# Routing start of a hybrid attention/mLSTM/MoE layer: out-projection tail in column quarters, split top-k, single bias products

## The chip, the cores and the metric

The kernel runs on one core of a Trainium2 chip, in float32. The metric is the device time of one execution in microseconds (us). The kernel before took 1073.36 us, the median of 3 runs (1073.18 to 1074.63).

## The reference, cut to what matters

One layer over 256 tokens (two tiles of 128, t = 0 and 1) of width 1024. Attention and mLSTM give `mixed`; then:

```python
x = x + jnp.einsum('bse,ed->bsd', mixed, w_out[l])               # the out-projection
h = rmsnorm(x, norm2_g[l])
logits = jnp.dot(h, w_router) + b_router                         # 32 experts
top_v, top_e = lax.top_k(logits, 4)
gates = jax.nn.softmax(top_v, axis=-1)
# each expert e, on the tokens that chose it:
gu = jnp.dot(xb, w_gate_up[e]) + b_gate_up[e]                    # 1024 -> 2048
act = min(gu[:, :1024], 7) * sigmoid(1.702 * gate) * (clip(up) + 1)
y = jnp.dot(act, w_down[e]) + b_down[e]                          # 1024 -> 1024
x = x + sum of gate * y
```

The weights of the 32 experts are 32 times (8.39 + 4.19) MB = 402.7 MB, each read once.

## The kernel before, in words

Weights pass through `ring`, 12 pieces of 2 MB in SBUF. An expert takes four gate/up pieces (`load_gu`, L398) and two down pieces (`load_d`, L410). All are issued by SyncE in one fixed order; from expert 2 on each issue waits until TensorE has used the piece that held the slot (`gu_used`, `d_used`). Experts 0 and 1 are loaded while the mixer still runs. The last two pieces of expert 1 go to slots 10 and 11, which hold the second half of `w_out` and the turned activations `ht`: slot 10 waits for `mixed` 4 (all of the out-projection done), slot 11 for `logit_parts` 2 (`ht` read). Then comes the bias row of expert 2 (`load_brow`, L402, behind `brow_used`), and then the first gate/up piece of expert 2, behind `gu_used` 1. That semaphore rises when TensorE has done the first two k blocks of expert 0's gate/up products (L1493).

The stretch that the change touches lies between the mixer and that product. Order on TensorE (PE), written out by hand: `out_half(t, c, ks)` (L1311) multiplies tile t by column half c of `w_out`, 512 columns a product; the first four k blocks of all four halves are done earlier, k 4 to 7 from 141 us. Between them `turn_x(t, i)` (L1333) transposes four 128-column blocks of the new x. Then `logit_part` (L1344) forms the router logits: eight k blocks go to four 32-row strips of one bank as 32-wide products, the strips are copied out (`part_copy`, ScalarE L713), and `fold_parts` (L1354) adds them by one product with a folding matrix. `tint_first(h)` (L1362) starts bank h with expert 0's gate/up bias, two one-row products each. Then the ranks (L1387, L1388, L1391), one product whose result nobody reads (L1389), `gather_first` (L1412: the picked tokens, eight products of 256 columns), `turn_rows` (L1433) and `gate_up` (L1493).

VectorE (DVE) adds the out-projection to x (`add_x`, L966), sums squares (L970), copies tile 1's transposed blocks (`turned_1`, L974), then runs for each tile the chain logits, MAX8, index, compare, reduce (L994 to L1004) that gives `mask`, and after both tiles `pos` (L1017) and `pick` (L1007) for each. ScalarE (ACT) squares (L693), takes Ln and Exp (L699, L701) for the norm factor `rs2`, copies tile 0's transposed blocks (L708) and the parts (L713), takes the softmax exponentials (L723), loads a table (L730) and copies the first half of the gathered rows (L732). Engines work in order, each instruction behind its waits.

Of the kernel before, what the change touches and what calls it, by code (L numbers as in the profile page):

```python
# [28 lines left out]
P = 128  # L29
# [81 lines left out]
def layer_kernel(nc, x, norm1_g, w_in, q_norm_g, k_norm_g, conv_w, conv_b, w_mq, w_mk, b_igate, b_fgate,  # L111
                 mh_norm_g, w_out, norm2_g, w_router, b_router, w_gate_up, b_gate_up, w_down, b_down,
                 attn_bias, out):
    with ExitStack() as ctx:
# [113 lines left out]
        ss2h = sb("ss2h", [P, T, 2])  # L228
        ss2 = sb("ss2", [P, T])
# [18 lines left out]
        ld_small = sem("ld_small")  # L248
# [10 lines left out]
        ld_g2 = sem("ld_g2")  # L259
# [14 lines left out]
        eps_ready = sem("eps_ready")  # L274
# [38 lines left out]
        m_arg1 = sem("m_arg1")  # L313
# [13 lines left out]
        mixed = sem("mixed")  # L327
        x1_ready = sem("x1_ready")
# [11 lines left out]
        top_found = sem("top_found")  # L340
        eq_ready = sem("eq_ready")
# [17 lines left out]
        fold_ready = sem("fold_ready")  # L359
# [36 lines left out]
        def _(sp):  # L396
# [24 lines left out]
            sp.dma_start(bif[:, 0:1], b_igate[0].rearrange("(h o) -> h o", o=1)).then_inc(ld_small, 16)  # L421
            sp.dma_start(bif[:, 1:2], b_fgate[0].rearrange("(h o) -> h o", o=1)).then_inc(ld_small, 16)
# [4 lines left out]
            for r, g in ((R_QG, q_norm_g), (R_KG, k_norm_g)):  # L427
                for i in range(2):
# [9 lines left out]
                         norm2_g[0].rearrange("(q p j) -> p q j", p=P, j=RUN)).then_inc(ld_g2, 16)  # L438
# [24 lines left out]
            sp.wait_ge(mixed, 4)  # L463
            load_d(1, 0, 10)
            sp.wait_ge(logit_parts, T)
# [97 lines left out]
        def _(act_e):  # L563
# [5 lines left out]
            for t in range(T):  # L569
                act.wait_ge(ld_x[t], 16)  # L570
                if t:
                    act.wait_ge(x_ms, t)
                act.activation(sq_x, xres[:, t, :], ACT.Square, accum_out=ss1[:, t:t + 1]).then_inc(x_ms, 1)
                act.wait_ge(x_ms, t + 1)
                act.wait_ge(eps_ready, 1)
# [120 lines left out]
            def rms_x(t):  # L696

                act.wait_ge(ss2_sum, t + 1)
                act.activation(rs2[:, t:t + 1], ss2[:, t:t + 1], ACT.Ln, scale=1.0 / D, bias=eps[:, 0:1]).then_inc(act_step, 1)  # L699
                act.wait_ge(act_step, 7 + t)  # L700
                act.activation(rs2[:, t:t + 1], rs2[:, t:t + 1], ACT.Exp, scale=-0.5).then_inc(x1_rs, 1)  # L701
# [3 lines left out]
            rms_x(0)  # L705
# [4 lines left out]
            def part_copy(t):  # L710

                act.wait_ge(logit_parts, t + 1)
                act.activation(part_t[:, t, :], bank[ACC[t]][:, 0:P], ACT.Copy).then_inc(part_read, 1)  # L713
# [79 lines left out]
        def _(dve):  # L793
# [10 lines left out]
            dve.memset(eps[:, :], EPS).then_inc(eps_ready, 1)  # L804
            dve.wait_ge(consts, 1)
            dve.tensor_reduce(fold[:, :], ident[:, :].rearrange("p (g e) -> p e g", e=NE), AX.X, ALU.add).then_inc(fold_ready, 1)
# [37 lines left out]
            dve.wait_ge(ld_small, 16 * 2)  # L844
# [57 lines left out]
            def decay(h):  # L902

                a_bc = bank[6 + h // 2][:, (h % 2) * SEQ:(h % 2 + 1) * SEQ]
                dve.tensor_scalar(e_m[:, h, 0:SEQ], a_bc, acol[:, 0, 0, h:h + 1], 0.0, ALU.subtract, ALU.max)\
                    .then_inc(m_arg1, 1)
                dve.wait_ge(m_arg1, h + 1)
# [60 lines left out]
            def sum_x(t):  # L968
                dve.wait_ge(x1_ss, 2 * t + 2)
                dve.tensor_tensor(ss2[:, t:t + 1], ss2h[:, t, 0:1], ss2h[:, t, 1:2], ALU.add).then_inc(ss2_sum, 1)  # L970

            def turned_1(i):
                dve.wait_ge(h2_turned, 3 + i)
                dve.tensor_copy(ht[:, 4 * i:4 * i + 4, P:SEQ], bank[6 + i][:, :].rearrange("p (k n) -> p k n", k=4))\  # L974
                    .then_inc(turned_x1, 1)


            dve.wait_ge(ld_wr, 32)
# [12 lines left out]
            for t in range(T):  # L991
# [7 lines left out]
                dve.max_index(top_i[:, t, :], top_v[:, t, :], lg[:, t, :]).then_inc(top_found, 1)  # L999
                dve.wait_ge(top_found, t + 1)  # L1000
                dve.tensor_tensor(eq[:, t], expert_no[:, :].unsqueeze(1).broadcast_to([P, TOPK, NE]),
                                  top_i[:, t, 0:TOPK].unsqueeze(2).broadcast_to([P, TOPK, NE]), ALU.is_equal).then_inc(eq_ready, 1)
                dve.wait_ge(eq_ready, t + 1)
                dve.tensor_reduce(mask[:, t, :], eq[:, t].rearrange("p j e -> p e j"), AX.X, ALU.add).then_inc(mask_ready, 1)  # L1004
            dve.tensor_scalar(nv0[:, :], top_v[:, :, 0], -1.0, None, ALU.mult).then_inc(top_ready, 1)
# [9 lines left out]
            for t in range(T):  # L1015
# [3 lines left out]
                take_half(0, t).then_inc((picked_t0, picked)[t], 1)  # L1019
            dve.wait_ge(top_exp, T)  # L1020
# [39 lines left out]
            def experts(base, flagged=None):  # L1060
                dve.wait_ge(xr_turned, base + 1)
                if flagged:
                    dve.wait_ge(ld_g2, 16)
# [37 lines left out]
        def _(pe):  # L1101
# [49 lines left out]
            pe.wait_ge(ld_vec, 16 * 8)  # L1151
# [157 lines left out]
            def out_half(t, c, ks):  # L1309
                for k in ks:  # L1310
                    mm = pe.matmul(bank[ACC[2 * t + c]][:, :], mix_t[:, k, t * P:(t + 1) * P], wout[k // 4][:, k % 4, c * BANK:(c + 1) * BANK],  # L1311
                                   start=(k == 0), stop=(k == KD - 1))
# [23 lines left out]
            def logit_part(t, half):  # L1336

                if t == 0 and half == 0:
                    pe.wait_ge(wr_ready, 1)
                    pe.wait_ge(x1_ready, 2)  # L1340
                pe.wait_ge((turned_x0, turned_x1)[t], half + 1)
                for g in range(4):
                    k = 4 * half + g
                    mm = pe.matmul(bank[ACC[t]][g * NE:(g + 1) * NE, 0:P], wr[:, k, :], ht[:, k, t * P:(t + 1) * P],  # L1344
                                   start=(half == 0), stop=(half == 1), skip_group_check=True)
                if half:
                    mm.then_inc(logit_parts, 1)

            def fold_parts(t):

                pe.wait_ge(part_read, t + 1)
                if t == 0:
                    pe.wait_ge(fold_ready, 1)
                pe.matmul(bank[ACC[t]][:, SEQ:SEQ + NE], part_t[:, t, :], fold[:, :], start=True, stop=True).then_inc(logits, 1)  # L1354

            def tint_first(h):

                if h == 0:
                    pe.wait_ge(ld_brow[tint(0)], 16)
                for c in range(2):  # L1360
                    i = 2 * h + c
                    mm = pe.matmul(bank[h][c * CAP:(c + 1) * CAP, :], ones[32 * i:32 * i + 1, 0:CAP],  # L1362
                                   brow[32 * i:32 * i + 1, tint(0), :], start=True, stop=False, skip_group_check=True)
                if h:
# [19 lines left out]
            tint_first(1)  # L1384
            fold_parts(1)
            pe.wait_ge(mask_ready, 1)
            pe.matmul(bank[RANK[0]][:, 0:NE], before, mask[:, 0, :], start=True, stop=True).then_inc(ranks, 1)  # L1387
            pe.matmul(bank[RANK[1]][:, 0:NE], ones[:, :], mask[:, 0, :], start=True, stop=False)  # L1388
            pe.matmul(bank[ACC[3]][:, 0:SEQ], ones[:, :], xres[:, 0, 0:SEQ], start=True, stop=True)  # L1389
# [36 lines left out]
            def turn_rows(n, src, first=False):  # L1426
# [7 lines left out]
                mm.then_inc(xr_turned, 1)  # L1434

# [177 lines left out]
```

## Time and profile before

| | |
|---|---|
| median of 3 runs | 1073.36 us |
| the profiled execution | 1073.03 us |
| its span | 1071.2 us |
| PE busy, DVE busy, ACT busy | 98%, 18%, 13% of the span |
| read from HBM | 423.31 MB |

The profiled execution took 1073.03 us, of which 1071.2 us is the span from its first to its last recorded instruction. Busy shares are averages over stages with different limits. A float32 product appears in the trace as two matmul records, so "x16" on a product line is 8 products; a transpose is one record.

### The profile page before, as it was taken

What the parts mean: (1) busy time and instruction counts of PE and PEld (TensorE: products, weight loads), DVE (VectorE), ACT (ScalarE), POOL (GpSimd) and SP (SyncE); (2) the same over time, 40 slices, a digit from 0 to 9 for tenths busy, and PEclk for the clock granted to TensorE, in tenths of its full rate; (3) what the DMA queues carried; (4) which work ended last, traced back from release to release, by engine and by line L of the source; (5) the groups of instructions that cost most, each with busy time, mean ns of one, the idle gap of its engine ahead of it and who ended that gap; (6) DMA issues with size and microseconds to landing.
All of it is one profiled execution on the core that took longest, in us unless ns stands there. A gap on an engine that the chain in (4) does not pass through costs nothing.

```text
span 1071.2 us, 12026 instructions
## 1 busy us (share of the span) xinstructions
PE 1044.9 (98%) x4795; PEld 391.2 (37%) x4795; DVE 192.6 (18%) x470; ACT 140.8 (13%) x294; POOL 5.2 (0%) x22
## 2 busy tenths in 40 slices
PE   9999999999999999999999999999999999999997
PEld 5655543333333333333333333333333332333332
DVE  2143323111111111111111111111111110101111
ACT  2134421000111001111111111111110010001101
POOL 1000000000000000000000000000000000000000
PEclk9999999999999999999999999999999999999999
DMA  9952598999999999999999999999999999999995
GB/s 345 362 203 79 207 393 342 429 427 427 428 427 429 429 428 426 430 427 429 426 429 428 428 428 429 429 427 427 429 427 427 428 429 429 427 428 430 423 428 233
DMA packets 40491, 424.63 MB, mean 396 GB/s; under 512 B 6384, under 2 KB 7448, under 8 KB 15640
## 3 DMA queue, kind: packets, MB, share of 16 engines
q1 hardware_dynamic: 40456, 424.37, 94.6%
q8 instruction: 13, 0.21, 0.1%
q14 instruction: 6, 0.05, 0.0%
q10 hardware_dynamic: 16, 0.00, 0.0%
HBM read 423.31 MB, written 1.05 MB: 396 GB/s over the span
## 4 chain that ended last, share of the span: by engine, by line
PE 75%; SPq 13%; DMA 9%; issue 1%; DVE 0%; ACT 0%; another core or an unknown queue 0%; DVEq 0%
PE bank L1493 31%; PE bank L1526 16%; DMA ring<-in_w_gate_up 9%; SPq L398 6%; PE bank L1125 5%; SPq L410 5%; PE bank L1456 4%; PE bank L1422 4%; PE bank L1311 3%; PE bank L1401 2%; SPq L402 2%; PE bank L1433 2%; PE bank L1511 2%; PE bank L1147 1%; PE bank L1159 1%
## 5 line engine op out<-in xcount | busy, mean ns | idle before, releaser
L1493 PE MATMUL bank<-ring,xe_t 128*64 128x512 f32 x2048 | 450.5, 595 | 14.0 <-DMA ring<-in_w_gate_up 13.5
L1493 PEld LDWEIGHTS bank<-ring,xe_t 128*64 128x64 f32 x2048 | 142.6, 137 | 318.3 <-issue 287.9
L1526 PE MATMUL bank<-ring,late 128*64 128x512 f32 x992 | 219.9, 595 | 0.6 <-DMA ring<-in_w_down 0.6
L1048 DVE TENSOR_SCALAR gate_c<-bank 128x512 f32<-128x512 f32 x32 | 22.1, 692 | 648.1 <-PE bank L1493 648.1
L1526 PEld LDWEIGHTS bank<-ring,late 128*64 128x64 f32 x992 | 68.8, 137 | 127.6 <-issue 124.0
L739 ACT ACTIVATE s_sb<-bank 128x256 f32<-128x256 f32 x32 | 12.3, 384 | 467.9 <-PE bank L1502 467.9
L1456 PE MATMUL bank<-late,s_sb 64*128 64x512 f32 x256 | 63.6, 615 | 0.8 <-ACT late L755 0.8
L1422 PE MATMUL bank<-xres,pick 128*64 128x512 f32 x248 | 60.1, 605 | 0.0
L1125 PE MATMUL bank<-ring 128*128 128x512 f32 x128 | 58.9, 600 | 0.0
L755 ACT ACTIVATE late<-bank 128x512 f32<-128x512 f32 x32 | 19.1, 597 | 229.2 <-PE bank L1526 229.2
L1033 DVE TENSOR_TENSOR xe_t<-bank,g_run 128x512 f32<-128x512 f32 (+1 forms) x33 | 22.2, 676 | 87.5 <-PE bank L1433 87.5
L1401 PE MATMUL bank<-brow,ones 1*64 1x512 f32 x248 | 33.7, 613 | 0.0
L1125 PEld LDWEIGHTS bank<-ring 128*128 128x128 f32 x128 | 22.9, 190 | 24.7 <-issue 24.7
L1456 PEld LDWEIGHTS bank<-late,s_sb 64*128 64x128 f32 x256 | 22.0, 186 | 22.6 <-issue 20.9
L1422 PEld LDWEIGHTS bank<-xres,pick 128*64 128x64 f32 x248 | 15.0, 136 | 41.2 <-issue 41.2
L728 ACT ACTIVATE late<-bank 128x512 f32<-128x512 f32 x31 | 18.5, 597 | 85.9 <-PE bank L1422 85.9
L1311 PE MATMUL bank<-ring 128*128 128x512 f32 x64 | 28.4, 594 | 1.0 <-ACT ring L685 1.0
L1511 PEld LDWEIGHTS bank<-ident,up_c 128*128 128x128 f32 x128 | 17.9, 209 | 26.0 <-issue 25.1
L1511 PE MATMUL bank<-ident,up_c 128*128 128x128 f32 x128 | 24.0, 310 | 0.0
L1433 PE MATMUL bank<-ident,late 128*128 128x128 f32 x124 | 23.1, 309 | 0.6
L1052 DVE SCALAR_TENSOR_TENSOR up_c<-up_c,gate_c 128x512 f32<-128x512 f32 x32 | 22.1, 691 | 1.2
L1055 DVE TENSOR_TENSOR up_c<-up_c,sig_g 128x512 f32<-128x512 f32 x32 | 22.1, 692 | 1.1
(206 smaller groups left out, 438.5 us busy)
## 6 DMA issues: line engine op xcount, KB each, us to landing
ring<-in_w_gate_up SPq DMA_DIRECT2D x128, 2048.0 KB, 37.6
ring<-in_w_down SPq DMA_DIRECT2D x63, 2048.0 KB, 36.0
ring<-in_w_in SPq DMA_DIRECT2D x5, 2048.0 KB, 15.3
ring<-in_w_out SPq DMA_DIRECT2D x2, 2048.0 KB, 10.2
ring<-in_w_in SPq DMA_DIRECT2D x2, 1024.0 KB, 8.4
ring<-in_w_down SPq DMA_DIRECT2D x2, 1024.0 KB, 46.1
ring<-in_attn_bias SPq DMA_DIRECT2D x1, 1536.0 KB, 18.4
xres<-in_x SPq DMA_DIRECT2D x2, 512.0 KB, 3.8
```

The costliest lines, as they stand in the source:

```text
L398: sp.dma_start(gu_half(s), w_gate_up[0, e, h * RUN * P:(h + 1) * RUN * P, :].rearrange("(p j) n -> p j n", j=RUN))\
L410: sp.dma_start(down_piece(s), rows).then_inc(ld_piece[s], 16)
L1033: return dve.tensor_tensor(xe_t.rearrange("p (c b) n -> p c b n", c=2)[:, :, lo:hi, :], bank[7][:, :].rearrange("p (b c n) -> p c b n", b= ...
L1125: mm = pe.matmul(dst[:, :], ht[:, k, t * P:(t + 1) * P], win[:, b % WINS, k, :], start=(k == 0), stop=(k == KD - 1))
L1311: mm = pe.matmul(bank[ACC[2 * t + c]][:, :], mix_t[:, k, t * P:(t + 1) * P], wout[k // 4][:, k % 4, c * BANK:(c + 1) * BANK], start=(k == ...
L1401: mm = pe.matmul(bank[h][c * CAP:(c + 1) * CAP, :], ones[32 * i:32 * i + 1, 0:CAP], brow[32 * i:32 * i + 1, u, :], start=True, stop=False, ...
L1422: mm = pe.matmul(bank[7][c * CAP:(c + 1) * CAP, :], pick[:, t, :], xres[:, t, c * BANK:(c + 1) * BANK], start=(t == 0), stop=(t == T - 1), ...
L1433: mm = pe.transpose(bank[7][:, b * P:(b + 1) * P], runs[:, b // RUN, b % RUN, :], ident[:, :])
L1456: mm = pe.matmul(bank[ACC[2 * t + c]][:, :], s_sb[c * CAP:(c + 1) * CAP, u, t * P:(t + 1) * P], y_sb[c * CAP:(c + 1) * CAP, :], start=Fals ...
L1493: mm = pe.matmul(bank[h][c * CAP:(c + 1) * CAP, :], xe_t[:, k, :], w[:, k % RUN, at:at + BANK], start=False, stop=(k == KD - 1), skip_grou ...
L1511: mm = pe.transpose(dst[:, j * P:(j + 1) * P], act_runs[:, j, :], ident[:, :])
L1526: mm = pe.matmul(dst[c * CAP:(c + 1) * CAP, :], turned[:, at:at + CAP], w[:, k % DRUN, c * BANK:(c + 1) * BANK], start=(k == 0), stop=(k = ...
```

## The change

- The last half of tile 1's out-projection (columns 512 to 1023) is done as two column quarters of 256. Its early part (k 0 to 3) still comes as one product series in bank 5; the second quarter's part of it is added to x ahead (`x1_split`), and its k 4 to 7 go to bank 0.
- Tile 0's top-k chain (`route(0)`) and its pick (`first_pick(0)`) are put ahead on VectorE: `route(0)` before the addition of the last quarter, `first_pick(0)` before `route(1)`.
- Of tile 1's logits, k 0 to 5 go through the strips and the fold; k 6 and 7 are added onto the folded logits by two products of 32 columns.
- The four bias products are called one by one: 0 and 1 (both in bank 0) before the last rank product, 2 after `gather_first`, 3 after the transposes of the gathered rows. The unread product L1389 is gone.
- The copies of tile 1's first six transposed blocks move from VectorE to ScalarE; its part copy moves from ScalarE to VectorE. The sum of squares of tile 1 goes through the bias of Identity and Ln on ScalarE, without VectorE.
- SyncE waits for `mixed` 5 (was 4) and for `logits` 2 (was `logit_parts` 2) ahead of the last two pieces of expert 1. Some semaphores are merged (`ld_small` into `ld_vec`, `ld_g2` into `ld_wr`, `eps_ready` and `fold_ready` into `dve_consts`).

```diff
 # SyncE
-            sp.wait_ge(mixed, 4)
+            sp.wait_ge(mixed, 5)
             load_d(1, 0, 10)
-            sp.wait_ge(logit_parts, T)
+            sp.wait_ge(logits, T)
             load_d(1, 1, 11)
 # ScalarE
             square_x(1, 0)
-            part_copy(0)
-            square_x(1, 1)
-            rms_x(1)
-            part_copy(1)
+            act.wait_ge(x1_ss, 3)
+            act.activation(ss2[:, 1:2], ss2h[:, 1, 0:1], ACT.Identity, scale=1.0 / D, bias=eps[:, 0:1]).then_inc(act_step, 1)
...
+            square_quarter(0)
+            act.wait_ge(h2_turned, 3)
+            act.activation(ht[:, 0:4, P:SEQ], bank[6][:, :].rearrange("p (k n) -> p k n", k=4), ACT.Copy).then_inc(turned_x1, 1)
+            act.activation(ss2q[:, 2:3], ss2q[:, 0:1], ACT.Identity, scale=1.0 / D, bias=ss2[:, 1:2]).then_inc(act_step, 1)
+            act.wait_ge(h2_turned, 4)
+            act.activation(ht[:, 4:6, P:SEQ], bank[7][:, 0:SEQ].rearrange("p (k n) -> p k n", k=2), ACT.Copy).then_inc(turned_x1, 1)
+            square_quarter(1)
...
 # VectorE
             add_x(0, 0)
             add_x(0, 1)
-            sum_x(0)
+            dve.wait_ge(half_mixed, 1)
+            dve.tensor_tensor(last, bank[ACC[3]][:, SEQ:2 * SEQ], last, ALU.add).then_inc(x1_split, 1)
...
             add_x(1, 0)
-            turned_1(0)
-            add_x(1, 1)
-            sum_x(1)
-            turned_1(1)
...
+            add_quarter(0, bank[ACC[3]])
+            route(0)
+            dve.wait_ge(x1_split, 1)
+            add_quarter(1, bank[0])
+            dve.wait_ge(logit_parts, 2)
+            dve.tensor_copy(part_t[:, 1, :], bank[ACC[1]][:, 0:P]).then_inc(part_read, 1)
+            dve.wait_ge(h2_turned, 5)
+            dve.tensor_copy(ht[:, 6:KD, P:SEQ], bank[7][:, SEQ:2 * SEQ].rearrange("p (k n) -> p k n", k=2)).then_inc(turned_x1, 1)
+            first_pick(0)
+            route(1)
...
+            first_pick(1)
 # TensorE
             turn_x(0, 0)
-            out_half(1, 0, range(4, KD)).then_inc(mixed, 1)
+            out_half(1, 0, range(4, 6))
             turn_x(0, 1)
-            out_half(1, 1, range(4, 6))
+            out_half(1, 0, range(6, KD)).then_inc(mixed, 1)
+            logit_part(0, range(4), 1)
+            logit_part(0, range(4, KD), 2)
+            pe.wait_ge(x1_split, 1)
+            out_quarter(0, range(4, KD)).then_inc(mixed, 1)
             turn_x(1, 0)
-            out_half(1, 1, range(6, KD)).then_inc(mixed, 1)
-            logit_part(0, 0)
-            logit_part(0, 1)
-            logit_part(1, 0)
-            turn_x(1, 1)
-            fold_parts(0)
-            tint_first(0)
-            logit_part(1, 1)
-            tint_first(1)
-            fold_parts(1)
+            out_quarter(1, range(4, 6))
+            turn_quarter(0)
+            fold_parts(0).then_inc(logits, 1)
+            out_quarter(1, range(6, KD)).then_inc(mixed, 1)
+            logit_part(1, range(4), 1)
+            logit_part(1, range(4, 6), 2)
+            turn_quarter(1)
...
+            fold_parts(1)
+            pe.wait_ge(turned_x1, 3)
+            for k in (6, 7):
+                mm = pe.matmul(bank[ACC[1]][:, SEQ:SEQ + NE], ht[:, k, P:SEQ], wr[:, k, :], start=False, stop=(k == KD - 1),
+                               skip_group_check=True)
+            mm.then_inc(logits, 1)
             pe.matmul(bank[RANK[1]][:, 0:NE], ones[:, :], mask[:, 0, :], start=True, stop=False)
-            pe.matmul(bank[ACC[3]][:, 0:SEQ], ones[:, :], xres[:, 0, 0:SEQ], start=True, stop=True)
+            tint_first(0)
+            tint_first(1)
...
+            tint_first(2)
...
                 mm.then_inc(xr_turned, 1)
+                if first:
+                    tint_first(3)
```

## Rows read from the trace of the kernel before

**Rows 1.** The page, part 1: busy us, share of the span, instructions.

```profile
PE 1044.9 (98%) x4795; PEld 391.2 (37%) x4795; DVE 192.6 (18%) x470; ACT 140.8 (13%) x294; POOL 5.2 (0%) x22
```

**Rows 2.** Windows: stretch, length, busy by engine, granted PE clock, DMA share, GB/s.

```profile
155.00:160.00 5.00, 5.00 (x50) 2.08 (x48) 3.00 (x10) 1.66 (x6) 0.00 (x0) 1.00 0.86 249
...
165.00:170.00 5.00, 4.48 (x22) 1.79 (x20) 1.82 (x5) 0.38 (x1) 0.00 (x0) 0.85 0.60 257
170.00:175.00 5.00, 5.00 (x31) 1.58 (x29) 1.47 (x6) 0.28 (x1) 0.00 (x0) 1.00 0.55 154
...
500.00:700.00 200.00, 199.87 (x948) 68.34 (x946) 30.23 (x63) 19.52 (x35) 0.00 (x0) 1.00 1.01 428
```

**Rows 3.** Timeline of SyncE's issues: start us, us, engine, line, what.

```profile
156.35 3.32 SPq L410 DMA_DIRECT2D ring<-in_w_down  x2
...
171.46 11.33 SPq L398 DMA_DIRECT2D ring<-in_w_gate_up  x4
```

**Rows 4.** Timeline near the end, TensorE; idle before and its releaser in brackets.

```profile
1049.97 3.65 PE L1526 MATMUL bank<-ring,late 128*64 128x512 f32 x16 [0.56 <-DMA ring<-in_w_down]
...
1054.88 3.65 PE L1526 MATMUL bank<-ring,xe_t 128*64 128x512 f32 x16 [1.25 <-DMA ring<-in_w_down]
```

**Rows 5.** Chain that ended last, in order: start us, us, what.

```profile
141.00 7.13 PE bank L1311 x16
148.14 0.44 PE bank L1333 x4
...
154.60 1.72 PE bank L1311 x4
156.32 0.79 PE bank L1344 x24
...
157.91 1.00 PE bank L1362 x4
...
160.27 0.35 PE bank L1354 x2
...
160.65 0.26 DVE sig_g L994
...
161.79 0.37 DVE sig_g L1004
...
162.73 3.35 PE bank L1412 x16
166.08 1.04 PE bank L1433 x4
...
167.62 3.65 PE bank L1493 x16
...
183.72 1.87 PE bank L1422 x8
```

**Rows 6.** Timeline of VectorE and ScalarE around the change.

```profile
156.36 0.69 DVE L966 TENSOR_TENSOR xres<-bank,xres 128x512 f32<-128x512 f32 x1 [1.03 <-PE bank L1311]
...
157.14 0.62 ACT L693 ACTIVATE sig_g<-xres 128x512 f32<-128x512 f32 x1
...
158.40 0.20 ACT L701 ACTIVATE rs<-rs 128x1 f32<-128x1 f32 x1
...
159.34 0.28 ACT L713 ACTIVATE gate_c<-bank 128x128 f32<-128x128 f32 x1 [0.73 <-PE bank L1344]
...
162.95 1.28 ACT L730 ACT_TABLE_LOAD   x1
...
165.27 0.38 ACT L732 ACTIVATE up_c<-bank 128x256 f32<-128x256 f32 x1 [1.03 <-PE bank L1412]
```

**Rows 7.** Windows of half a microsecond, columns as in Rows 2.

```profile
163.00:163.50 0.50, 0.50 (x6) 0.34 (x4) 0.43 (x3) 0.50 (x1) 0.00 (x0) 0.61 0.93 393
...
166.50:167.00 0.50, 0.50 (x3) 0.31 (x2) 0.50 (x2) 0.00 (x0) 0.00 (x0) 0.98 1.22 524
```

**Rows 8.** Chain, earlier: 32 products of 256 columns.

```profile
41.28 14.01 PE bank L1159 x64
```

More of the change, by code:

```diff
@@ L327, in layer_kernel @@
         mixed = sem("mixed")
+        x1_split = sem("x1_split")
         x1_ready = sem("x1_ready")
@@ L694, in square_x, with square_quarter @@
                                accum_out=ss2h[:, t, c:c + 1]).then_inc(x1_ss, 1)
[L696 to L701, printed above, removed]
+            def square_quarter(q):
+                act.wait_ge(x1_ready, 4 + q)
+                act.wait_ge(x1_ss, 3 + q)
+                act.activation(squares[:, SEQ:2 * SEQ], xres[:, 1, BANK + q * SEQ:BANK + (q + 1) * SEQ], ACT.Square,
+                               accum_out=ss2q[:, q:q + 1]).then_inc(x1_ss, 1)
             square_x(0, 0)
             square_x(0, 1)
-            rms_x(0)
+            act.wait_ge(ss2_sum, 1)
+            act.activation(rs2[:, 0:1], ss2[:, 0:1], ACT.Ln, scale=1.0 / D, bias=eps[:, 0:1]).then_inc(act_step, 1)
+            act.wait_ge(act_step, 7)
+            act.activation(rs2[:, 0:1], rs2[:, 0:1], ACT.Exp, scale=-0.5).then_inc(x1_rs, 1)
             for i in range(2):
@@ L982, in _, with route @@
             add_x(0, 1)
-            sum_x(0)
+            last = xres[:, 1, BANK + SEQ:2 * BANK]
+            dve.wait_ge(half_mixed, 1)
+            dve.tensor_tensor(last, bank[ACC[3]][:, SEQ:2 * SEQ], last, ALU.add).then_inc(x1_split, 1)
+            dve.wait_ge(x1_ss, 2)
+            dve.tensor_tensor(ss2[:, 0:1], ss2h[:, 0, 0:1], ss2h[:, 0, 1:2], ALU.add).then_inc(ss2_sum, 1)
             add_x(1, 0)
-            turned_1(0)
-            add_x(1, 1)
-            sum_x(1)
-            turned_1(1)
+            add_quarter(0, bank[ACC[3]])
             dve.engine_nop().then_inc(gu_read, 1)
-            for t in range(T):
+            def route(t):
+                if t == 0:
+                    dve.wait_ge(x1_ss, 3)
                 dve.wait_ge(logits, t + 1)
@@ L1013, in take, with first_pick @@
                 ins.then_inc(picked, 1)
-            for t in range(T):
+            def first_pick(t):
                 dve.wait_ge(ranks, t + 1)
@@ L1311, in out_half, with out_quarter @@
                     mm = pe.matmul(bank[ACC[2 * t + c]][:, :], mix_t[:, k, t * P:(t + 1) * P], wout[k // 4][:, k % 4, c * BANK:(c + 1) * BANK],
-                                   start=(k == 0), stop=(k == KD - 1))
+                                   start=(k == 0), stop=(k == KD - 1 or 2 * t + c == 3), skip_group_check=True)
+                return mm
+            def out_quarter(q, ks):
+                at = BANK + q * SEQ
+                for k in ks:
+                    mm = pe.matmul((bank[ACC[3]], bank[0])[q][:, 0:SEQ], mix_t[:, k, P:2 * P], wout[1][:, k % 4, at:at + SEQ],
+                                   start=(q == 1 and k == 4), stop=(k == KD - 1), skip_group_check=True)
                 return mm
@@ L1352, in fold_parts, with tint_first @@
                 if t == 0:
[L1353 to L1358, printed above, removed]
-                    pe.wait_ge(ld_brow[tint(0)], 16)
[L1360 to L1364, printed above, removed]
+                    pe.wait_ge(dve_consts, 2)
+                return pe.matmul(bank[ACC[t]][:, SEQ:SEQ + NE], part_t[:, t, :], fold[:, :], start=True, stop=(t == 0),
+                                 skip_group_check=True)
+            def tint_first(i):
+                if i == 0:
+                    pe.wait_ge(ld_brow[tint(0)], 16)
+                h, c = i // 2, i % 2
+                mm = pe.matmul(bank[h][c * CAP:(c + 1) * CAP, :], ones[32 * i:32 * i + 1, 0:CAP],
+                               brow[32 * i:32 * i + 1, tint(0), :], start=True, stop=False, skip_group_check=True)
+                if i == 3:
                     mm.then_inc(brow_used, 1)
```

90 lines of the change are left out of this document (46 added, 44 removed).

## The prediction

> **What bounds the kernel.** The page gives PE 98% of the span [rows 1], which suggests a kernel bound by TensorE. The windows by stage say otherwise: between 500 and 700 us the DMA share is 1.01 at 428 GB/s [rows 2], so the transfer of weights is full while PE is merely close behind. 32 experts carry 402.7 MB; at 428 GB/s one expert (12.58 MB) takes 29.4 us. At the end PE waits for pieces again: the products at 1049.97 and 1054.88 follow DMA landings, and lie 4.91 us apart, which is one 2 MB piece at 428 GB/s (2.10 MB / 428 = 4.9) [rows 4]. So the end is the end of the stream of weights, plus a tail that the change leaves alone.
>
> The reader should then ask when that stream became unbroken. The windows show two holes: the DMA share is 0.86 in 155 to 160, then 0.60 in 165 to 170 and 0.55 in 170 to 175 [rows 2]. The first ends with the issue of slot 10 at 156.35, when the out-projection is done; the second ends with the first gate/up piece of expert 2, issued at 171.46 [rows 3]. That issue waits for the first 8 products of expert 0, 167.62 + 3.65 = 171.27 [rows 5]. From there 30 experts, 377.5 MB, must flow: 377.5 / 0.428 = 882 us, which from about 172.5, a microsecond behind the issue, gives 1054.5. The trace has the last-but-one piece at 1054.88 and so the last at about 1059.8; the 5 us between are 0.6% of the stream, which the rate lacks over so long a way. So every microsecond by which L1493 begins earlier than 167.62 ends the kernel one earlier, as long as slots 10 and 11 are filled by then. In the second hole the DMA has about (1 - 0.60 + 1 - 0.55) x 5 = 4.3 us free, so a shift of 1 or 2 us is not caught by it.
>
> **The change, step by step.** I rebuild the time at which L1493 starts. PE's last stretch begins at 141.00.
>
> 1. Out-projection tail. Both halves of tile 0: 7.13 -> 148.13. Transposes (0,0) 0.44, k 4 and 5 of half (1,0) 1.72, transposes (0,1) 0.44, k 6 and 7 1.72 -> 152.45. Logits of tile 0, 8 of the 12 products that took 0.79: 0.53 -> 152.98. Quarter 0: a product of 256 columns costs 14.01 / 32 = 0.438 [rows 8], four are 1.75 -> 154.73; transposes (1,0) 0.44 -> 155.17; two products of quarter 1 0.88 -> 156.05; two transposes 0.22, fold 0.14; two products 0.88 -> 157.29 [rows 5]. Before, the same point was 154.60 + 1.72 = 156.32. The out-projection therefore ends 0.97 later. Slot 10 is issued that much later (about 157.3), and its 2 pieces would be in at about 1 us later than before, by 169.5, still ahead of the next issue near 170. Cost on the end: 0; if L1493 started over 2 us earlier, that would be the new cover lost.
> 2. VectorE. Tile 0's logits are folded at 156.41. From L994 to the mask the chain takes 161.79 + 0.37 - 160.65 = 1.51 [rows 5], so `route(0)` runs from 156.45 to 157.99. Queued behind it is the addition of quarter 1, ready at 157.33: it starts 0.7 late. A 512-wide addition takes 0.69 [rows 6]; half the width I take as 0.42 (bounds 0.35 and 0.69) -> 158.44. Before, the last addition ended at 156.36 + 0.69 = 157.05. So x is complete 1.4 later. For it wait the last two transposes, the last square and through them the norm factor.
> 3. What comes after is shorter. Two transposes -> 158.95 (ready 0.5 after the addition); the copy of 256 columns, 0.42 -> 159.40; meanwhile the mask of tile 0 gives its rank product, and the fold of tile 1 (its copy done at 158.74) is out of the way by 159.3. The two products of k 6 and 7 are no row of this trace. The fold, one product of the same shape, took 0.35 with its load [rows 5]; two take 0.35 to 0.70, I take 0.65 as their weights are two full loads -> 160.10. The norm factor was ready at 158.40 + 0.20 after an addition that ended at 157.05, 1.55 later [rows 6]; with 256 instead of 512 squares and without VectorE's sum it is 1.25 -> 159.7, in time. `first_pick(0)` fills VectorE from 159.43 to 159.97, also in time. `route(1)` starts at 160.13, before at 160.65: 0.5 earlier. That is about the stall that the bias product caused: tile 1's part copy was finished at 159.34 + 0.28 = 159.62 [rows 6], and the fold could start only at 160.27, when the second pair of bias products ended. Mask of tile 1: 161.64.
> 4. Bias products 0 and 1 take 1.00 together (157.91; a like pair stands at 159.27) [rows 5] and lie in `route(1)`: 160.3 to 161.3, hidden. The unread product is gone, also hidden before. The rank, `pos` and `pick` of tile 1 keep their 0.57 before L1412 could have all it needs: pick 1 done at 162.68, before 163.20.
> 5. The gather. Before, its first half waited for both masks too and ran from 162.73. Now pick 0 is long ready, so the first four products start right after the last rank product, at 161.85. The work is 1.87 at full clock (the same columns in 183.72) but took 3.35 [rows 5], because the granted clock fell to half at about 163.1 and came back at about 166.5 [rows 7]: 1.2 instead of 2.4 GHz. PE had been mostly waiting, with short products only, in the stretch before it fell. At full clock the gather ends at 161.85 + 1.87 = 163.7, before 166.08.
> 6. Bias product 2 follows. Alone it still takes a whole product's time, 0.9 to 1.0 [rows 5], -> 164.6. Behind it wait the transposes; but the copy of the first rows waits for ScalarE's table load, which shifts from 162.95 to about 162.55, + 1.28 = 163.85, + 0.38 [rows 6] -> 164.3. Cost on the path about 0.3. Transposes and the multiplication into `xe_t`: before 1.04 and 0.50 (166.08 to 167.62); at full clock 0.6 and 0.5. Bias product 3 stands between, 165.2 to 166.15, and outlasts the 0.5 by 0.45. L1493 starts at 166.15: 1.47 earlier. With the clock at half from 163.1 to 166.5 the same steps give: gather end 164.4, product 2 at 166.2, transposes 166.8, product 3 at 167.8: 0.15 later than before.
>
> The clock is thus the largest term, about 1.6 us. There is a second way to get most of it: PE waits from 157.7 to 158.5 and around 159, so the clock may fall earlier, at about 160, and be back at about 163. Then only bias products 0 and 1 (1.9 instead of 1.0, to about 162.4) and the start of the gather run at half speed. Pick 1 is then at 163.4, gather end 164.7, product 2 165.6, transposes 166.2, L1493 at 167.15: 0.45 earlier.
>
> The Trainium skill ("TensorE: Matmul & The Clock Gate", Part 1) adds that the low clock is the default, that activity lifts it, and that the point of the switch differs between runs of the same kernel. By that rule the earlier or later fall is decided by chance of phase and not by this order of work, and a low clock through both is possible too; one trace of before cannot show it.
>
> Forecast: between these two, L1493 about 0.95 earlier; 1073.03 - 0.95 = 1072.1 for an execution like the profiled one. The median of the runs stands 0.33 above the profiled one, so 1072.4.
>
> The remaining edits cost nothing: merged semaphores wait for small loads that were issued at the start; the ACT copies (tile 1, 0.6 and 0.4) end by 157.1, before PE asks for them at 157.3; slot 11's issue moves from about 159.4 to 160.1 while slot 10 is still flowing until about 163; expert 2's bias row comes behind bias product 3, near 166, ahead of the piece at 170. If that row were late it would hold the first piece: 0.6 for its issue, no more.
>
> **Rivals.**
> - Full gain, clock never low in the routing: L1493 at 166.15, 1073.36 - 1.5 = 1071.9. For it: bias products 0 and 1 and half of the gather now fill the stretch that was empty before the fall. Against: new waits at 157.7 and 159.
> - The gain is eaten: clock low exactly over the gather as before, products 2 and 3 at half speed on the path. 1073.36 + 0.15 = 1073.5.
> - Slower: the clock falls after the waits of 157.7 to 159.4 and stays low through the gather. The gather starts at 162.6 at half speed and ends at 166.3, product 2 at 167.2, transposes 167.8, product 3 168.7: 1.1 later, 1074.5. It decides as soon as the granted clock is 0.5 both at 161 and at 165. Product 3 alone then costs more than all that the order saves.
> - The reorder doesn't shorten the routing: the addition of quarter 1 behind `route(0)` sits later than I have it, or k 6 and 7 with their loads take over 1.1, and `route(1)` begins at or after 160.65. Then only the clock is left: 1072.5 to 1074.
>
> **Chances.** Forecast (gain 0.4 to 1.3) 0.35; full gain or more 0.27; eaten or no shorter routing 0.25; slower by about 1 us or more 0.13. From the median, 0.2% is 2.1 us, about what a measurement of this kernel can tell from no change. Only a full gain with cheaper steps than mine passes it (0.1), and only the slower rival with further late steps (0.06). The range goes from the full gain with the low bounds of steps 2, 3 and 6 (0.9 less) to the slower rival: 1071.0 to 1074.5.
>
> **What would show it.** Right: L966's last addition near 158.4; `route(1)` near 160.1; L1412 from about 161.9 and ending before 165; L1493's first product 0.4 to 1.5 before 167.62, SyncE's first L398 after it by 3.8, and the end moved by as much; the granted clock at 1.0 for most of the gather. Wrong: a DMA share under 1 after 175 us, or an end that does not follow L1493; `route(1)` after 160.65; a shift of L1493 of over 2 us either way.

## The result, and the profile after

The changed kernel takes 1075.89 us (median of 20 runs, 1073.35 to 1079.32) against 1073.96 for the kernel before (20 runs). Three runs of the kernel before here (1207, 1346 and 3852 us) and one of d_full_late below (1347 us, at a clock of 0.751) are slow executions that the ratios and the mean clocks leave out; without them the median before is 1073.63. The ratio is 1.0021, 95% interval 1.0013 to 1.0029: 0.2% slower. The prediction said 1072.4 with a range of 1071.0 to 1074.5.

The chain of the changed kernel, as in [rows 5] (start us, us, what). L1337 is the quarter products, L1425 the two products of k 6 and 7, L1453 the gather, L1395 a bias product, L1474 the transposes and L1536 the gate/up products.

```profile
140.94 7.13 PE bank L1330 x16
...
152.38 0.58 PE bank L1377 x16
152.96 1.92 PE bank L1337 x8
...
158.07 0.42 DVE xres L978
...
158.54 0.46 PE bank L1366 x2
...
159.50 0.65 PE bank L1425 x4
...
160.16 0.26 DVE sig_g L1002
...
161.30 0.38 DVE sig_g L1012
...
162.15 3.50 PE bank L1453 x16
165.65 1.00 PE bank L1395 x2
166.65 0.68 PE bank L1474 x4
167.32 1.00 PE bank L1395 x2
168.32 5.28 PE bank L1536 x16
```

Up to the mask of tile 1 the reorder does what it says: the top-k chain of tile 1 starts at 160.16, before at 160.65. The gather ends at 165.65, before at 166.08. Then it turns: from the gather's end to L1536 pass 2.67 us, before 1.54, and the first 8 gate/up products take 5.28 instead of 3.65. The two bias products stand in the first stretch; the windows show the clock of the second (columns as in [rows 2]; the granted clock is the third figure from the right):

```profile
162.00:165.00 3.00, 3.00 (x16) 1.72 (x17) 1.17 (x5) 1.78 (x6) 0.00 (x0) 0.50 1.03 434
...
165.50:168.50 3.00, 3.00 (x12) 1.12 (x12) 1.80 (x5) 0.00 (x0) 0.00 (x0) 1.00 0.98 421
...
169.00:172.00 3.00, 3.00 (x8) 0.73 (x6) 0.00 (x0) 0.00 (x0) 0.00 (x0) 0.50 0.05 19
```

The clock is at 1.2 GHz not once, as in [rows 7], but twice: over the gather (162.0 to 165.5), and again over the gate/up products (168.9 to 172.2). While it is low the second time the DMA share is 0.05: the stream of weights stands still and waits for PE. SyncE's issues (as in [rows 3]):

```profile
157.52 2.98 SPq L406 DMA_DIRECT2D ring<-in_w_down  x2
168.50 0.57 SPq L398 DMA_DIRECT2D brow<-in_b_gate_up  x1
173.79 11.33 SPq L394 DMA_DIRECT2D ring<-in_w_gate_up  x4
```

The first gate/up piece of expert 2 is issued 2.33 us later than before (171.46), and the last-but-one piece of the kernel comes 3.09 later, 1057.97 against 1054.88 [rows 4]:

```profile
1057.97 3.65 PE L1569 MATMUL bank<-ring,xe_t 128*64 128x512 f32 x16 [1.24 <-DMA ring<-in_w_down]
```

The 0.76 us between these two arise in the stream, and no run here says how.

The runs are spread over 6 us, and the mean granted clock that each lists goes with the time: 7 runs at 0.998 lie between 1073.35 and 1074.84, 6 runs at 0.993 between 1078.29 and 1079.32 (correlation over the 20 runs: -0.97). A mean clock of 0.993 instead of 0.998 is 0.005 x 1074 = 5.4 us of full clock lost, and the means of the two groups differ by 4.6 us. The profile above, at 0.996, is a middle one, and the question became which part of the change holds the clock down.

### The profile page after: what moved, and what is told of

Its sections match the earlier page's. It is cut to its first block, busy times and chain, and to the rows that moved or that the text cites. A ratio compares the mean times of both kernels' runs of the same rounds, so it can differ in the third digit from the quotient of the medians.

```text
span 1074.2 us, 12047 instructions
## 1 busy us (share of the span) xinstructions
PE 1047.4 (97%) x4801; PEld 392.9 (37%) x4801; DVE 192.4 (18%) x471; ACT 141.9 (13%) x299; POOL 5.2 (0%) x22
## 4 chain that ended last, share of the span: by engine, by line
PE 72%; SPq 15%; DMA 10%; issue 1%; DVE 1%; ACT 0%; another core or an unknown queue 0%; DVEq 0%
PE bank L1536 30%; PE bank L1569 15%; DMA ring<-in_w_gate_up 9%; SPq L394 7%; SPq L406 6%; PE bank L1144 5%; PE bank L1499 4%; PE bank L1463 4%; PE bank L1330 2%; SPq L398 2%; PE bank L1442 2%; PE bank L1474 2%; PE bank L1554 1%; PE bank L1166 1%; PE bank L1178 1%
## 5 line engine op out<-in xcount | busy, mean ns | idle before, releaser
L1536 PE MATMUL bank<-ring,xe_t 128*64 128x512 f32 x2048 | 452.4, 597 | 14.1 <-DMA ring<-in_w_gate_up 14.1
L1536 PEld LDWEIGHTS bank<-ring,xe_t 128*64 128x64 f32 x2048 | 142.9, 137 | 320.6 <-issue 288.3
L1144 PE MATMUL bank<-ring 128*128 128x512 f32 x128 | 58.9, 600 | 0.0
L1330 PE MATMUL bank<-ring 128*128 128x512 f32 x56 | 24.8, 594 | 1.0 <-ACT ring L681 1.0
L1474 PE MATMUL bank<-ident,late 128*128 128x128 f32 x124 | 23.1, 309 | 0.6
```

The lines of the kernel that those rows point to most:

```text
L1144: mm = pe.matmul(dst[:, :], ht[:, k, t * P:(t + 1) * P], win[:, b % WINS, k, :], start=(k == 0), stop=(k == KD - 1))
L1474: mm = pe.transpose(bank[7][:, b * P:(b + 1) * P], runs[:, b // RUN, b % RUN, :], ident[:, :])
L1536: mm = pe.matmul(bank[h][c * CAP:(c + 1) * CAP, :], xe_t[:, k, :], w[:, k % RUN, at:at + BANK], start=False, stop=(k == KD - 1), skip_grou ...
```

## The experiments

From a_bias_early on, every kernel is compared with the kernel before on the same chip (medians there 1073.97 to 1074.18). Medians of kernels that ran on different chips are compared by their ratios. "Mean clock" is the mean over the runs of the granted clock that each lists. "Issue" is the time of SyncE's first gate/up piece of expert 2 in the profiled execution, whose own time stands beside it.

| kernel | median us | ratio (95% interval) | mean clock of its runs | issue, time of profiled run |
|---|---|---|---|---|
| before | 1073.96 | 1 | 0.9972 | 171.46, 1073.03 |
| changed | 1075.89 | 1.0021 (1.0013 to 1.0029) | 0.9959 | 173.79, 1076.03 |
| after_again | 1076.68 | 1.0016 (1.0002 to 1.0029) | 0.9958 | 172.36, 1073.49 |
| a_bias_early | 1073.21 | 0.9995 (0.9984 to 1.0005) | 0.9972 | 174.08, 1075.50 |
| b_before_late | 1077.19 | 1.0037 (1.0024 to 1.0050) | 0.9948 | 174.08, 1075.48 |
| d_full_late | 1074.87 | 1.0004 (0.9995 to 1.0013) | 0.9973 | 173.39, 1074.43 |
| m_only_two_late | 1075.29 | 1.0012 (0.9997 to 1.0028) | 0.9961 | 172.04, 1073.62 |
| n_only_three_late | 1074.49 | 0.9998 (0.9985 to 1.0012) | 0.9965 | 176.30, 1079.03 |
| h_after_unread | 1074.41 | 1.0009 (0.9999 to 1.0020) | 0.9972 | 177.76, 1079.12 |
| g_after_fill_two | 1074.48 | 1.0003 (0.9994 to 1.0012) | 0.9975 | 175.38, 1076.80 |
| e_fill | 1072.00 | 0.9980 (0.9971 to 0.9989) | 0.9993 | 170.14, 1071.99 |
| k_early_fill_two | 1071.84 | 0.9981 (0.9973 to 0.9990) | 0.9989 | 171.03, 1072.52 |
| q_rows_1_late | 1073.87 | 1.0001 (0.9992 to 1.0009) | 0.9982 | 171.22, 1072.71 |
| r_rows_128_late | 1072.25 | 0.9987 (0.9978 to 0.9996) | 0.9990 | 170.26, 1071.62 |
| f_before_fill | 1073.78 | 0.9999 (0.9990 to 1.0008) | 0.9975 | 171.82, 1074.77 |
| o_before_bias_moved | 1074.82 | 0.9998 (0.9988 to 1.0008) | 0.9971 | 173.55, 1074.78 |

The last column bears out what the prediction took as the bound: from 170.14 to 177.76 the time follows the issue (7.62 us of issue, 7.13 of time; correlation over the 16 profiled executions 0.97). Measured from the kernel before, 14 of them lie within 0.7 us of "as much later as the issue"; n and f end 1.2 and 1.4 us later than that, and why is open. One caution on single profiles: PE's last stretch, which starts at 141.00 in the kernel before, starts anywhere from 140.92 to 141.78 in these executions, ahead of all that was edited. A start that is 0.6 to 0.8 late (a, e, f, h, n, o, q) shifts every later time of that profile.

**a_bias_early.** All four bias products before the last rank product.

```diff
             tint_first(0)
             tint_first(1)
+            tint_first(2)
+            tint_first(3)
             pe.wait_ge(mask_ready, 2)
...
             gather_first()
-            tint_first(2)
...
                 mm.then_inc(xr_turned, 1)
-                if first:
-                    tint_first(3)
```

> The changed kernel with bias products 2 and 3 laid beside 0 and 1, before the last rank product; all else as changed. Theory 1 (the two late single products are the loss): the gather still ends near 165.6 if the clock is low over it, but the gate/up products (L1536) start 1.1 us sooner than 168.32, near 167.2, and at full clock, so 3.65 instead of 5.28 for the first 8 products; first gate/up piece of expert 2 issued near 171.0 to 171.3; median 1072.7 to 1073.7, the same as the kernel before or up to 1.3 us under it. Theory 2 (the new waits of the quarters and the tile-0 top-k let the clock fall, late products matter little): second fall of the clock over the gate/up products stays, mean granted clock 0.996 or less, median above 1074.8.

Median 1073.21, 12 runs from 1071.04 to 1076.44. As Theory 1 has it, the loss is gone: the ratios differ by 0.26%, and their intervals lie apart. The times that Theory 1 gave for the trace did not come: in the profiled execution the clock is low without a break from 161.8 to 172.0, the first gate/up products take 5.37 and the issue is at 174.08. So the late products are not the only thing that goes with a low clock: Theory 2 holds for a part of the runs (4 of 12 at 0.995 or less).

```profile
163.50:168.00 4.50, 4.50 (x20) 2.06 (x16) 1.84 (x6) 1.45 (x2) 0.00 (x0) 0.50 0.99 421
```

In this stretch stand the gather and the transposes, full-height work alone, with no gap on PE, and the clock stays low all the same. A low clock that does not come back is therefore no sign of one-row products.

**b_before_late.** The kernel before, bias products 2 and 3 laid a second time where the change has them.

```diff
             gather_first()
+            again(2)
             turn_rows(0, up_c, first=True)
...
                 mm.then_inc(xr_turned, 1)
+                if first:
+                    again(3)
```

> The kernel before with bias products 2 and 3 laid a second time, singly, after the gather and after the transposes of the gathered rows (same values again, result unchanged); all else as before. Theory 1: the gap from the gather's end to L1493 grows from 1.54 us (166.08 to 167.62) to about 2.7, the first products may run at half clock; median 1 to 3 us above before, so 1075 to 1077, with a wide spread between runs. Theory 2: the additions hide in the waits of the transposes and cost under 0.5 us: median under 1074.5.

Median 1077.19 of 5 runs, 3.2 us above before. From the gather's end to the gate/up products (L1501 here) pass 2.67 us, and these take 5.28. The same two numbers as in the changed kernel, without its quarters and without its early top-k:

```profile
162.76 3.18 PE bank L1418 x16
165.94 1.00 PE bank L1394 x2
166.94 0.68 PE bank L1439 x4
167.62 1.00 PE bank L1394 x2
168.61 5.28 PE bank L1501 x16
```

**d_full_late.** a_bias_early with two unread products at the late places, as long but 128 rows high.

```diff
+            pe.matmul(bank[6][0:CAP, :], ones[:, 0:CAP], xres[:, 0, 0:BANK], start=True, stop=True, skip_group_check=True)
```

> As a_bias_early, but at the two late places stand two unread products of the same length (512 columns, 64 wide) that read 128 rows instead of 1. It tells the length of the late products from their height. If the clock counts one-row products as good as idle: the delay of 1.1 us stays (L1536 near 168.3 with the clock low over the gather) but the first gate/up products run at full clock, 3.65; median 1073.8 to 1074.8, mean clock 0.998. If only the delay and not the height matters for the clock: the first products at half clock as in the changed kernel, 5.3, mean clock 0.996, median near 1075.9.

Median 1074.87. Apart from the run of 1347 us none of its runs is under 0.996, and the first gate/up products take 3.43. In its profile the delay stays (L1538 at 169.76, the clock low from 160.9 to 167.6) and the second fall does not come. Its interval just touches that of the changed kernel, so alone it does not settle what the height does; q and r below were made for that.

**e_fill.** a_bias_early with unread products of 256 columns in PE's waits, four of them.

```diff
             logit_part(1, range(4, 6), 2)
+            pe.matmul(bank[ACC[3]][:, 0:SEQ], ones[:, :], xres[:, 0, 0:SEQ], start=True, stop=True)
```

(and the same before `mask_ready` 2, after `gather_first` and after the transposes, the last two into bank 6)

> As a_bias_early, with unread products of 256 columns (0.44 us) in PE's four waits: after tile 1's logit parts, before the last rank product, after the gather, after the transposes. If a low clock over the gather is what is left, and filling the waits holds the clock: gather at full clock (1.9 instead of 3.5), L1536 near 165.7 to 166.2, first piece of expert 2 issued near 169.7, median 1071.3 to 1072.3, mean clock 1.000. If the clock falls by something that fillers don't change: no better than a_bias_early, or 0.5 us worse.

Median 1072.00, 0.20% under before and faster than both kernels, 1.2 under a_bias_early, which differs only in lacking the fillers; 10 runs within 1.9 us. The clock is never low in its profile, and the gather takes 1.88:

```profile
162.81 1.88 PE bank L1457 x16
164.69 0.63 PE bank L1627 x2
165.32 0.48 PE bank L1478 x4
...
166.30 3.65 PE bank L1540 x16
```

**f_before_fill, g_after_fill_two, h_after_unread, k_early_fill_two** are read together. f is the kernel before with three more such products: one beside L1389 before the last rank product, one after the gather, one after the transposes. g is the changed kernel, late bias products kept, with the two ahead of the gather. h is the changed kernel with L1389 alone put back. k is e_fill without the two behind the gather.

> The kernel before with unread products of 256 columns in its own waits: a second one beside L1389 before the last rank product, one after the gather, one after the transposes. Theory: the low clock over the gather cost it 1.5 us; kept at the upper level the gather ends near 164.6, L1493 starts near 166.1 to 166.3, median 1.3 to 1.6 under before. That would mean that the reorder of the change is itself worth next to nothing once the clock is held. Rival: the reorder is worth its 0.5 us, and this kernel stays 0.5 us slower than e_fill (which ran 2.0 under before).

> The changed kernel with its late single bias products kept, and two unread products of 256 columns ahead of them: after tile 1's logit parts and before the last rank product. If the clock before the gather decides all: gather at full clock, ends near 163.8, L1536 near 166.2, first products 3.65, median 1071.8 to 1072.5, as e_fill. If the one-row products themselves let the clock fall: first gate/up products at half clock (5.3), median 1073.5 to 1075 and a spread of over 3 us.

> The changed kernel with the unread product (old L1389) put back in its old place, nothing else. If taking it out is what let the clock fall more often: median within 0.5 us of before, 1073.5 to 1074.5, and fewer runs with a mean clock of 0.993. If the late bias products are: median stays above 1075.

> All four bias products early, and only the two unread products ahead of the gather (e_fill without the two behind it). If those behind it aren't needed: L1536 starts 0.2 to 0.5 us sooner than e_fill's 166.30, median 1071.5 to 1072.0, mean clock 1.000. If they are: the clock falls over the gate/up products in part of the runs, median above 1072.5 with a spread of over 3 us.

f gained nothing (ratio 0.9999): in its profile the clock still fell, at 161.7, and the fillers, then mostly at half speed (0.94 and 0.85), stood before the last rank product: the gather started at 163.84. So it doesn't tell what the reorder is worth under a held clock.

g stays at 1.0003, 2.6 us over k on the same chip (95% interval of the difference of means, by resampling the runs: 1.8 to 3.5); the only difference is the place of bias products 2 and 3. The longer path explains about 1.1 of it (2.67 us from the gather's end to the gate/up products in after_again, 1.52 in k). The mean clocks, 0.9975 and 0.9989, differ by 0.0014 x 1074 = 1.5 us. This is the first of two pairs that carry the argument. g's profiled execution has the late ones at 1.90 each and the gate/up products at 4.99.

h lies between before and the changed kernel (1.0009). Its median is where its expectation put the rival, that taking L1389 out let the clock fall more often; but its interval also reaches into that of the changed kernel (1.0013 to 1.0029), and two of its 12 runs are at 0.993 all the same. So whether taking L1389 out mattered stays open. Its profile is one of these two, and shows the worst case whole:

```profile
164.00 3.61 PE bank L1454 x16
167.62 1.90 PE bank L1395 x2
169.51 1.06 PE bank L1475 x4
170.57 1.90 PE bank L1395 x2
172.46 5.10 PE bank L1537 x16
```

```profile
162.00:166.00 4.00, 4.00 (x16) 1.75 (x14) 1.72 (x8) 1.95 (x5) 0.00 (x0) 0.50 1.00 424
166.00:170.00 4.00, 4.00 (x13) 1.32 (x10) 0.91 (x2) 0.38 (x1) 0.00 (x0) 0.50 0.97 418
170.00:174.50 4.50, 4.50 (x11) 1.22 (x11) 0.88 (x3) 0.00 (x0) 0.00 (x0) 0.50 0.02 5
```

PE has no gap, and the clock does not come back. As in a_bias_early, that holds for the full-height gather (3.61 instead of 1.88) and the gate/up products as well as for the two bias products between them, so this trace shows what a low clock costs and not what keeps it low. k is as fast as e (0.9981): the fillers behind the gather aren't needed for the median, although k's profiled execution still has the clock low over the gather (3.43).

**m_only_two_late, n_only_three_late, o_before_bias_moved, after_again.** m and n keep one of the two late bias products each. o is the kernel before with its bias pairs moved, four together, to just ahead of L1389.

```diff
 # o_before_bias_moved
             fold_parts(0)
-            tint_first(0)
             logit_part(1, 1)
-            tint_first(1)
             fold_parts(1)
...
+            tint_first(0)
+            tint_first(1)
             pe.matmul(bank[ACC[3]][:, 0:SEQ], ones[:, :], xres[:, 0, 0:SEQ], start=True, stop=True)
```

> The changed kernel with only bias product 2 late (after the gather); 3 is laid early beside 0 and 1. Theory (each late one-row product costs its own time on the path and keeps the clock down): about half of the 2.7 us between the changed kernel and a_bias_early, so a median 1 to 1.7 under after_again of this call, near 1074.5. Rival (only the one right ahead of the gate/up products matters, as it fills their wait): as a_bias_early, 1073.2.

> The changed kernel with only bias product 3 late (after the transposes); 2 is laid early. Theory: 1 to 1.7 under after_again, near 1074.5; 3 costs less than 2 at full clock (0.5 of it lies in a wait), as much at half clock. Rival (3 is the whole loss): as after_again.

> The kernel before with its four bias products moved together to just before the unread product L1389, behind the fold of tile 1; no quarters, no top-k ahead. The stall of 0.5 us ahead of the fold goes: fold near 159.7, top-k of tile 1 near 160.1 as in the changed kernel. If this is all that the reorder gains: median 0.3 to 0.8 under before or, if the clock falls less often, down to 1.5 under; then quarters and early top-k are worth nothing. If the clock falls earlier through the thinner stretch before the fold: the same as before.

> The changed kernel once more, on the chip of this call, to stand beside the two halves of its late bias products: ratio to before 1.001 to 1.003, spread from 1073 to 1079, about a third of the runs at a mean clock of 0.993.

after_again repeats the loss (1.0016; 3 of 12 runs at 0.994 or less). m and n have medians 1.4 and 2.2 us under it, in the order that the theory gives, but their intervals overlap with its own, and 5 of m's 12 runs are at 0.994 or less; the split between the two products stays open.

o removes the stall ahead of the fold. Its profiled execution began PE's last stretch 0.72 later than the kernel before (141.72 against 141.00). Tile 1's top-k starts at 160.71 (before 160.65), so 0.66 earlier by this measure, where the changed kernel gains 0.43 (160.16 from a stretch begun at 140.94). In these single profiles, moving the bias products alone thus wins as much there as the quarters and the early top-k do. It is not won on the path: the four bias products and the unread one now end after the mask of tile 1 (162.20), and the clock falls at 161.7 in the middle of them:

```profile
160.71 0.24 DVE L994 SCALAR_TENSOR_TENSOR sig_g<-bank,rs,up_c 128x32 f32<-128x32 f32 x1
...
161.48 1.65 PE bank L1362 x8
163.12 1.15 PE bank L1389 x2
164.28 0.27 PE bank L1391 x2
164.54 3.61 PE bank L1412 x16
```

At full clock these two groups took 1.02 and 0.63 in e_fill, so they would still have ended near 163.1, behind the mask.

after_again's profiled execution is the clearest view of the second fall. The gather runs at full clock, and the clock falls afterwards, at 167:

```profile
162.34 1.88 PE bank L1453 x16
164.22 1.00 PE bank L1395 x2
165.22 0.67 PE bank L1474 x4
165.89 1.00 PE bank L1395 x2
166.89 5.28 PE bank L1536 x16
```

```profile
164.00:166.50 2.50, 2.50 (x11) 0.93 (x8) 1.49 (x4) 0.36 (x1) 0.00 (x0) 1.00 1.00 426
166.50:167.00 0.50, 0.50 (x3) 0.18 (x4) 0.31 (x2) 0.00 (x0) 0.00 (x0) 0.96 0.99 426
167.00:170.00 3.00, 3.00 (x8) 0.74 (x8) 0.00 (x0) 0.00 (x0) 0.00 (x0) 0.50 0.75 319
```

Before the fall PE was busy without a gap (2.50 of 2.50), two thirds of it with one-row products. The changed kernel's first profile has the same: no gap from 165.50 to 168.50 at full clock, and the fall at 168.9.

**q_rows_1_late, r_rows_128_late.** k_early_fill_two with two unread late products of 512 columns. The two kernels differ in nothing but the rows of these products, and ran on the same chip side by side. The edit from q to r:

```diff
-            pe.matmul(bank[6][0:CAP, :], ones[0:1, 0:CAP], xres[0:1, 0, 0:BANK], start=True, stop=True, skip_group_check=True)
+            pe.matmul(bank[6][0:CAP, :], ones[:, 0:CAP], xres[:, 0, 0:BANK], start=True, stop=True, skip_group_check=True)
```

> k_early_fill_two (all bias products early, two unread products ahead of the gather) with two unread products of 512 columns, 64 wide and 1 row high, after the gather and after the transposes. Theory (one-row products keep PE occupied but let the clock fall as if it waited): the first gate/up products run at half clock in many runs, mean clock near 0.997, median 2 to 3 us above the 1071.8 of k_early_fill_two, so near 1074.3. Rival (only the length of the late products counts): the same time and the same mean clock as r_rows_128_late within 0.5 us.

> The same, with the two late unread products 128 rows high instead of 1; all else equal, the same length at either clock. Theory: they hold the clock, so only the length is left, 0.7 to 1.1 us: median 1072.6 to 1073.2, mean clock 0.999 and the first gate/up products at 3.65. Rival: as q_rows_1_late within 0.5 us.

1073.87 against 1072.25: 1.6 us for the rows alone. The ratios to before are 1.0001 and 0.9987, and their intervals overlap a little; compared directly, the means differ by 1.5 us (95% interval by resampling the runs: 0.6 to 2.4). The mean clocks, 0.9982 against 0.9990, make 0.9 us of that; 0.3 is path in the profiles (from the gather's end to the end of the first gate/up products 6.25 us in q, 5.96 in r). Both came out faster than expected (near 1074.3, and 1072.6 to 1073.2), and no run of q is under 0.996. r is 0.4 above k, less than its longer path. The rival, that only the length counts, falls. Neither profiled execution shows a fall, so here it is the spread of runs and not a trace that carries the verdict; q's trace shows that two late one-row products can also pass at full clock:

```profile
164.80:168.50 3.70, 3.70 (x14) 1.32 (x16) 1.79 (x5) 0.11 (x1) 0.00 (x0) 1.00 1.01 430
```

## Why the prediction was wrong

**What bounds the kernel: right.** The time follows the issue of the first piece of expert 2, within 0.7 us in 14 of the 16 profiled executions.

**Steps 1 to 4: right.** Slot 10 issued at 157.52 (157.3 forecast), last addition ended at 158.49 (158.44), the two new products 0.65 (0.65), top-k of tile 1 at 160.16 (160.13), mask at 161.68 (161.64), its pick at 162.73 (162.68). The 0.5 us are there, 0.43 of them when the start of PE's last stretch is taken off (140.94 against 141.00). What they are due to is less than the prediction said: o has at least as much without quarters and early top-k.

**Step 6 failed, at the products behind the bias products.** The prediction priced bias products 2 and 3 by their own length, and let the issue move one for one with the start of the gate/up products, that is, took the first 8 of them at 3.65 in every case. The length of the bias products was right: in after_again, where the gather runs at full clock, the steps are 1.88, 1.00, 0.67, 1.00, so 2.67 us from the gather's end to L1536 where the sum had 2.45. But then the gate/up products take 5.28. L1536 starts 0.73 earlier than before (166.89), and its first 8 products end 0.90 later (172.17 against 171.27). The 1.63 us that the second low spell costs stood in no term, neither in the forecast nor in a rival. That products one row high, put there, make such spells more frequent or longer is what the pairs g against k and q against r show, over many runs. It is not so in each run: the clock also stays low without them (a_bias_early), and at full with them (q).

**Step 5 failed, in the place of the first spell.** The forecast lay between a clock that never falls here and one that is low from 160 to 163, so that most of the gather ran at full speed. In the changed kernel's profile it is low from 162.0 to 165.5, and the gather takes 3.50 instead of 1.87. Its start is 0.30 late too (162.15 against 161.85), as the last rank product itself takes 0.42. From the 166.15 of the full gain, 0.30, 1.63 and 0.22 for the later steps give the measured 168.32. The premise was also misread: the prediction has PE "mostly waiting" in the stretch before the old fall, but PE was busy for 2.25 of 3.00 us:

```profile
160.00:163.00 3.00, 2.25 (x15) 1.47 (x15) 2.21 (x12) 0.72 (x5) 0.00 (x0) 1.00 1.02 431
```

**The slower rival came nearest, and not by its mechanism.** It had the clock low at 161 already and through the gather, and back for good after it, and priced that at 1.1 us. In the changed kernel's profile the clock at 161 is 1.00, so its own sign did not appear; the first low spell lies over the gather alone, and 1.63 us of the 2.33 come from a second one that the rival did not have. In 6 of the 20 runs the loss is 4.7 to 5.7 us against the 1073.63 of the kernel before; none of these was profiled, but h_after_unread and n_only_three_late have profiled executions at the same mean clock of 0.993, and there the clock is low in one piece from 161.9 to 175.4 and from 161.6 to 175.2, over the gather, transposes, late bias products (1.90 each) and gate/up products. I gave the slower rival 0.13.

**The Trainium skill** ("TensorE: Matmul & The Clock Gate", Part 1) says that the point of the switch differs between runs of one kernel. The spread of 6 us that goes with the mean clock agrees. It also says that the gate goes by how busy the PE has been. PE's busy time alone does not show that here: in after_again the clock fell at 167.0 with PE busy 2.50 of 2.50 us up to 166.5.

What stays open: how much products 2 and 3 each cost; whether the removal of L1389 did harm; why the clock falls in one execution and not in the next; what quarters and early top-k are worth under a held clock, since the kernel before was not tried with fillers that stay off its path.

## What to carry to other kernels

Where PE's work thins out ahead of a dense stage, cost each product twice: by its time on the path, and by what it does to the granted clock of the stage behind it. Put one-row products (biases, broadcasts) where they run together and where full-height products stand around them, and fill PE's waits ahead of the dense stage with full-height ones. They took 1.2 us off here (e_fill against a_bias_early), and nothing off the kernel before, where they lay on its path. Look at the spread and the mean clock of many runs, since one profiled execution shows one of several outcomes.

## What the runs showed of the hardware

- Products one row high occupy TensorE and hold its clock less well than full-height ones: two late products of 512 columns 1 row high gave 1073.87 us at a mean clock of 0.9982 (q), 128 rows high 1072.25 at 0.9990 (r). With two such bias products in 3 us of unbroken work the granted clock fell at 167.0 (after_again); with two unread ones it stayed at 1.00 (q).
- Work without a gap does not by itself bring a low clock back soon: it stayed at 0.50 over 4.50 of 4.50 us of full-height products (a_bias_early, 163.5 to 168.0), and for 13.5 us in all in h_after_unread.
- Four one-row products of 512 columns that read rows 0, 32, 64 and 96 take 1.02 together at full clock (e_fill), one alone takes 1.00.
- The same program's time follows its mean granted clock almost exactly (correlation -0.97, 1073.35 at 0.998 to 1079.32 at 0.993), in a kernel whose end is set by its DMA stream: what the clock does between 160 and 176 us decides it.
